# Conditioning rows of a two-block transformer kernel: two column groups of 64 on TensorE against four of 32

## The reference

```python
cond = jax.nn.silu(c)                       # (1, 1024)
for l in range(DEPTH):                      # 2 layers
    ada = cond @ ada_w[l] + ada_b[l]        # ada_w[l]: (1024, 6 * 1024)
    sh1, sc1, g1, sh2, sc2, g2 = jnp.split(ada, 6, axis=-1)
    h = modulate(rmsnorm(x, norm_g[l, 0]), sh1, sc1)
    ...                                     # mixer (mLSTM, or latent attention)
    x = x + g1[:, None, :] * rmsnorm(y, norm_g[l, 1])
    h = modulate(rmsnorm(x, norm_g[l, 2]), sh2, sc2)
    y = sqrelu_mlp(h, mlp_w1[l], mlp_w2[l])
    x = x + g2[:, None, :] * rmsnorm(y, norm_g[l, 3])
# and kv_shift, kv_scale = split(cond @ kv_ada_w + kv_ada_b, 2)
```

## Time and profile before

| | |
|---|---|
| time, median of 3 runs | 1060.33 us |
| lowest, highest | 1058.5, 1061.13 us |
| span of the profiled execution | 1060.4 us |
| PE busy | 1011.3 us (95%) |
| PE weight loads busy | 879.9 us (83%) |
| DVE busy | 724.9 us (68%) |
| ACT busy | 531.2 us (50%) |
| moved by DMA | 205.42 MB, mean 194 GB/s |
| matmuls of line 592 | 160 records, 38.6 us busy |

### The profile page before, as it was taken

How to read it: one execution, slowest core, us unless ns; L and a number is a source line. 1 busy time by engine, 2 the same in 40 slices (tenths; PEclk the granted TensorE clock), 3 DMA queues, 4 the chain that set the end, 5 groups by cost and what they waited for, 6 DMA issues and landing times.

```text
span 1060.4 us, 19777 instructions
## 1 busy us (share of the span) xinstructions
PE 1011.3 (95%) x8530; PEld 879.9 (83%) x8530; DVE 724.9 (68%) x1194; ACT 531.2 (50%) x804; POOL 36.4 (3%) x33
## 2 busy tenths in 40 slices
PE   5999999889999999999999999999989899999997
PEld 4788899886888887887687999998678769999995
DVE  6789889518989776745766577665778765444544
ACT  3358432225734594563545555445646656445452
POOL 0000044100000100000000000000000000000000
PEclk9999999989999999999999999999989999999998
DMA  9664410432484452653445867777456266455420
GB/s 382 238 278 159 159 42 4 194 130 80 159 317 170 173 214 92 263 202 139 177 167 191 348 250 269 303 301 290 186 226 250 81 238 237 160 199 198 160 80 40
DMA packets 15223, 205.42 MB, mean 194 GB/s; under 512 B 1816, under 2 KB 1816, under 8 KB 2976
## 3 DMA queue, kind: packets, MB, share of 16 engines
q1 hardware_dynamic: 14544, 202.55, 50.3%
q10 hardware_dynamic: 592, 1.61, 0.5%
HBM read 203.10 MB, written 1.05 MB: 193 GB/s over the span
## 4 chain that ended last, share of the span: by engine, by line
PE 84%; DVE 10%; ACT 3%; issue 2%; DMA 1%; SPq 0%; DVEq 0%; ACTq 0%
PE bank L452 20%; PE bank L454 20%; PE bank L453 20%; PE bank L755 5%; PE bank L401 4%; DVE slot_parts L1910 2%; PE bank L658 1%; PE bank L559 1%; DVE arena L2387 1%; PE bank L736 1%; PE bank L631 1%; DVE arena L2375 1%; DMA pc<-in_params 1%; PE bank L620 1%; DVE arena L1853 1%
## 5 line engine op out<-in xcount | busy, mean ns | idle before, releaser
L452 PE MATMUL bank<-page_parts 128*128 128x512 f32 (+2 forms) x1254 | 430.4, 343 | 7.2 <-DVE page_parts L2193 2.3
L1910 DVE TENSOR_TENSOR slot_parts<-ring,page_parts 128x2048 fp32r<-128x2048 f32 (+2 forms) x121 | 271.4, 2254 | 139.0 <-ACT page_parts L1306 138.3
L1306 ACT ACTIVATE page_parts<-ring 128x2048 fp32r<-128x2048 f32 (+2 forms) x121 | 226.8, 1885 | 147.1 <-PE bank L454 91.2
L452 PEld LDWEIGHTS bank<-page_parts 128*128 128x128 f32 x1254 | 238.9, 191 | 34.1 <-issue 6.1
L454 PE MATMUL bank<-page_parts 128*128 128x512 f32 (+2 forms) x686 | 266.7, 389 | 0.0
L453 PE MATMUL bank<-slot_parts,page_parts 128*128 128x512 f32 (+2 forms) x686 | 266.6, 389 | 0.0
L453 PE MATMUL bank<-page_parts 128*128 128x256 f32 x568 | 160.7, 283 | 0.0
L454 PE MATMUL bank<-page_parts,slot_parts 128*128 128x256 f32 x568 | 160.7, 283 | 0.0
L454 PEld LDWEIGHTS bank<-page_parts 128*128 128x128 f32 x686 | 129.7, 189 | 26.5
L453 PEld LDWEIGHTS bank<-slot_parts,page_parts 128*128 128x128 f32 x686 | 130.0, 190 | 24.7
L1363 ACT ACTIVATE arena<-bank 128x512 f32<-128x512 f32 (+2 forms) x134 | 74.2, 575 | 131.7 <-PE bank L454 70.8
(11 more groups left out here) (298 smaller groups left out, 1147.9 us busy)
## 6 DMA issues: line engine op xcount, KB each, us to landing
ring<-in_stream SPq DMA_DIRECT2D x95, 2048.0 KB, 8.5
arena<-in_x SPq DMA_DIRECT2D x2, 512.0 KB, 4.3
arena<-in_gn ACTq DMA_DIRECT2D x2, 512.0 KB, 4.6
out<-arena SPq DMA_DIRECT2D x2, 512.0 KB, 2.6
cc<-in_consts SPq DMA_DIRECT2D x1, 899.0 KB, 6.5
small<-in_cond ACTq DMA_DIRECT2D x1, 512.0 KB, 10.0
pc<-in_params SPq DMA_DIRECT2D x1, 287.0 KB, 6.8
arena<-in_head_sel ACTq DMA_DIRECT2D x1, 32.0 KB
```

Of the source, the lines that this page charges most:

```text
L452: mm(out, a[0], b[0], start=start, stop=False)
L1306: act(unit_parts(n)[0], unit_values(n)[1], ACT.Copy).then_inc(ac.step("w_hi"), 1)
L1910: tt(unit_parts(n)[1], lo, hi, ALU.subtract).then_inc(dv.step("w_lo"), 1)
```

## The change

`ada_direct` now uses four groups of 32 columns: tile k goes to group k % 4, each group sums two tiles, and the bank holds four partial sums in its four quarters of 32 partitions. A constant column `quarter`, 1 in rows 0, 32, 64 and 96, takes the place of the column of `eye` in `ada_turned`, so that the turn adds four rows in place of two. The number of products stays as it is: eight in a panel, four in a turn. The block of constants grows from 1798 to 1799 columns. Nothing stands at another place in any engine's list.

```diff
@@ constants
-                        ("inv2", 32), ("zero", 1), ("eps", 1), ("kk_floor", 1), ("gn_eps", 1))
+                        ("inv2", 32), ("quarter", 1), ("zero", 1), ("eps", 1), ("kk_floor", 1), ("gn_eps", 1))
...
+    put("quarter", (p[:, None] % 32 == 0) * 1.0)
@@ ada_direct
                 for k in range(KT):
                     if pause and k == 5:
                         pe.wait_ge(*pause)
-                    group = slice(k % 2 * HD, (k % 2 + 1) * HD)
-                    ins = mm(b[group, :], cond[:, k:k + 1].to_broadcast([P, HD]), W[:, k, :], start=(k < 2), stop=(k >= KT - 2))
+                    group = slice(k % 4 * 32, (k % 4 + 1) * 32)
+                    ins = mm(b[group, :], cond[:, k:k + 1].to_broadcast([P, 32]), W[:, k, :], start=(k < 4), stop=(k >= KT - 4),
+                             tile_position=(0, k % 4 * 32))
@@ ada_turned
-                    ins = mm(b[:, ct * P:ct * P + 1], ada_row[:, ct * P:(ct + 1) * P], con("eye")[:, 0:1], start=True, stop=True)
+                    ins = mm(b[:, ct * P:ct * P + 1], ada_row[:, ct * P:(ct + 1) * P], con("quarter"), start=True, stop=True)
```

## The result

| | before | changed |
|---|---|---|
| median of 11 runs | 1061.4 us | 1068.25 us |
| lowest to highest | 1058.5 to 1065.4 us | 1063.26 to 1071.87 us |
| ratio | | 1.0057 (1.0041 to 1.0074) |
| span of the profiled execution | 1060.4 us | 1070.1 us |
| PE busy | 1011.3 us | 1006.7 us |

The change makes the kernel slower by 0.57%, some 6 us on the 1061.4 of before. The profiled execution of the changed kernel is the longest of its eleven (1071.87 us around its span), so its 9.7 us more of span are not the typical loss.

What follows compares the result with a forecast made beforehand. PE, 95% busy, was taken as the bound, with the panels as filler under a chain of DVE and ACT. 1060.4 us, 0 saved, plus 5 falls x 2.3 = 11.5 us lost gave 1072 us; range 1060 to 1080.

Steps and rivals of the forecast that it cites:

- Four groups at once: In each conditioning panel, 16 records run as four rounds of 0.43 us: 1.72 us, 1.71 us less per panel.
- Nothing of it on the path: At the six panel places PE finishes sooner but waits for the same DVE lines: 0 us saved.
- The falls: Longer PE idle at the six panel places drops the granted clock to half rate: 5 falls, 11.5 us lost.
- counted half: At the first two panel places, idle of 2.96 and 2.7 us: half a fall of the clock each.
- The fall at 781 us: Existing clock drop around PE's wait for `cq`, 6.8 us long, priced at 2.9 us; no gain from it forecast.
- The price: Cost of one clock fall behind a panel place: 2.3 us, the middle of 1.7 and 2.9.
- my lower bound: Least cost of one clock fall, 1.7 us, from the 3.2 us fall at 109 us.
- That the clock holds: Rival: at the panel places falls do not come or DVE's slack hides them; 1060 to 1063 us; chance 0.13.
- That the groups take turns: Rival: four groups run two by two, a panel stays at 3.4 us, time at 1060 us; chance 0.05.
- The stream: Rival: panel slots free 1.7 to 3.4 us sooner cut two landing waits, some 4 us: 1056 us; chance 0.04.
- The slower return of the clock: Rival: in DVE-paced stretches the clock recovers late; six falls at 2.9 us, 17.4 us, 1078 us; chance 0.1.

Runs made afterwards that it cites:

- The run with two tiles: Kernel before, two groups, only the first two of each conditioning panel's eight tiles computed: 1070.27 against 1060.53 us, ratio 1.0075.
- the filler: Kernel before plus four extra float32 products where PE waits for `cq` at 778 to 782 us: 1059.58 against 1062.57 us, ratio 0.9976.
- four groups twice: Changed kernel with each panel's eight products run twice, result unchanged: 1061.65 us against 1062.57 for the kernel before, ratio 0.9999.
- the first two places: Kernel before with four groups only at the first two of the six panel places (one panel each): ratio 1.0023.
- the third: Kernel before with four groups only at the third of the six panel places (two panels): ratio 1.0036.
- half of the filler: Changed kernel with each panel's first four tiles run once more ahead, 12 products: 1067.92 us against 1060.53 for the kernel before, ratio 1.0070.
- the last three places: Kernel before with four groups only at the last three of the six panel places (six panels): ratio 1.0037.
- half of the tiles: Kernel before, two groups, only four tiles per panel, five in panels with a pause: 1071.16 against 1062.57 us, ratio 1.0072.

## Why the prediction was right, and where a term was off

The forecast was 1072 us and 1068.25 us were measured. The mechanism holds, the size is too large: 11.5 us of loss were forecast, from the 1060.4 us of the profile. The eleven runs of before have a median of 1061.4 us, so 1 us of how near the two times lie is luck.

**Four groups at once: right.** I took 1.72 us for a panel's rounds, from the four tiles of line 736; the rows after have fours 0.43 us apart and 1.92 us with the tail. The yield that the Trainium skill gives for three column tiles ("TensorE: Matmul & The Clock Gate", Part 3), which I had weighed as 2.2 us, was not met here: nothing was lost with four. A panel takes 1.92 us with its tail.

**Nothing of it on the path: right.** The idle that I worked out was 2.96, 2.7, 4.2 and, around the pause, 2.5 and 1.5 us; measured were 2.97, 2.74, 4.25, 2.53 and 1.51 at the first four places, with the releasers of before. At the fifth only 0.65 us were left behind the pause, because the clock was low already and the last tiles took 1.93 us. The run with two tiles shows the same from the other side.

**The falls: right in kind, five forecast, six seen in the profiled execution.** Those with 2.97 and 2.74 us of idle, counted half, both came. Not every execution has them all: the second profile of the change has falls at five of the six places and none at the second, with the same idle of 2.74 us there. The fall at 781 us is another matter. In the changed kernel the wait of 2.22 us behind the transposes of `cq` left the clock alone:

```profile
788.20:791.40 3.20, 0.92 (x7) 1.00 0.55 236
```

Only the idle ahead of them had gone from 1.20 to 0.21 us. The profiles without the filler sort by this: the five with idle of 1.2 us and then 2.2 us there (before, four groups twice, the first two places, the third, half of the filler) have the fall, and the four with 0.2 and 2.2 us (both of the change, the last three places, two tiles) have none. With half of the tiles it was 0.38 and 2.31 us, and a fall of 3.4 us came at 793 us. My count of falls was a count of places, and had this one unchanged.

**The price: the step that was mis-sized.** I took 2.3 us for a fall, midway between 1.7 and 2.9. The four falls of 3.4 us cost 0.88 to 1.62 us, mean 1.37, below my lower bound. That bound was the whole half of a fall of 3.4 us, with PE full of work; but behind a place DVE still paces PE, and part of the lost rate goes into waits that are there anyway. At the second place the distance grew by only 0.88 us through a fall as long as the others, and there a later wait of 0.69 us for DVE (at line 462 of the kernel before) is gone. The fifth fall, 6.8 us long, cost 0.46 us for the same reason. Only the sixth, 10.2 us long, costs more than I took. The six together are 9.5 us in this execution, and the fall at 781 us, which my sum did not let go, gave 2.8 us back: 6.7 us. So the sum was too large by two terms, the price of a fall (2.3 us forecast, 1.6 us on average) and a gain put at nothing; that six falls came in place of five went the other way. Over all runs 11.5 us were forecast and 6 to 7 measured, which per place is about 1.1 us.

**The rivals.** That the clock holds was wrong: both profiles show it. That the groups take turns was wrong. The stream did not get ahead: SP's waits for the panels are 59.1 us in place of 68.7, but ACT's wait for landings hardly moved:

```profile
SPq L1244 <- PE bank L593: 59.1, 7, 47.7
...
ACT page_parts L1308 <- DMA ring<-in_stream: 52.2, 10, 7.4
```

Against the earlier trace rows that is 0.5 us of 52.7. The slower return of the clock happened at two of the six places (6.8 and 10.2 us) in both profiles.

The Trainium skill's rule that idle stretches between bursts bring the clock back to half ("TensorE: Matmul & The Clock Gate", "Why this matters for your kernels") agrees in direction with what was measured: removing idle at 781 us made the kernel faster (0.9976), and adding it in six places made it slower (1.0057).

## What to carry to other kernels

Before making an operation on TensorE shorter, look at what the engine waits for behind it. If it is another engine, the saving turns into idle time, and where a busy stretch follows, the clock may come back at half rate: here 16 us less of work (38.6 to 22.4 us) cost 6 us. The reverse holds too: a few products that nobody needs, put where TensorE waits ahead of a busy stretch, gained 0.2% here. Judge a clock effect by many runs, since one profile shows one draw of where the falls come, and in a profile by the distance between two fixed points of the work around the edit, since here up to 6 us of difference in span stood ahead of it.

## What was not expected

- Four column groups of 32, each with operands of the full 128 rows, run at once without any loss: 16 records of 512 float32 columns in 1.92 us, where one after the other would take 16 x 0.43 = 6.9 us.
- The low clock often begins after the idle is over, when PE is busy again: at 253.8 us, 1.3 us after PE resumed at 252.54, and at 571.2 us at the moment it resumed. The matmuls on either side of the first, from the timeline of the changed kernel:

```profile
253.55 0.39 PE L454 MATMUL bank<-slot_parts,page_parts 128*128 128x512 f32 x1
253.77 0.59 PE L455 MATMUL bank<-page_parts 128*128 128x512 f32 x1
254.16 0.63 PE L453 MATMUL bank<-page_parts 128*128 128x512 f32 x1
```

- Half of the missing filler put back did not help (1.0070), and leaving two tiles in place of four did not hurt more (1.0075 against 1.0072): the time lost is close to all or nothing, though the mean clock is not (0.982, 0.980 and 0.974).
- A fall can hide in another wait, and take a second fall away: the fifth place's 6.8 us at half rate cost 0.46 us, and with it the fall at 781 us went, which had cost 2.8.
